# Prompt rows' down projection as seven half-size products, with differences of weight quarters prepared in the value and convolution stages

## What is computed

```
def ffn_sublayer(h, prev, g, w_gu, conv_w, conv_b, w_down):
    gate, up = jnp.split(rms_norm(h, g) @ w_gu, 2, axis=-1)
    gate_c, state = causal_dwconv3(gate, prev, conv_w)
    return h + (jax.nn.silu(gate_c + conv_b) * up) @ w_down, state
```

## Time and profile before

| | us |
| --- | --- |
| median of 3 runs | 1823.1 |
| lowest and highest run | 1813.66, 1824.73 |
| profiled execution | 1823.89 |
| its span, first to last instruction | 1822.1 |
| mean granted TensorE clock | 0.949 of full speed |

### The profile page before, as it was taken

How to read it: one execution, slowest core, us unless ns; L and a number is a source line. 1 busy time by engine, 2 the same in 40 slices (tenths; PEclk the granted TensorE clock), 3 DMA queues, 4 the chain that set the end, 5 groups by cost and what they waited for, 6 DMA issues and landing times.

```text
span 1822.1 us, 34225 instructions
## 1 busy us (share of the span) xinstructions
PE 1681.8 (92%) x13965; PEld 1179.9 (65%) x14043; DVE 1112.3 (61%) x1906; ACT 811.9 (45%) x1483; POOL 732.7 (40%) x704
## 2 busy tenths in 40 slices
PE   6999999997776889989979997999999999999998
PEld 3644444444444665445568654788888888898897
DVE  5856665788797875356745337888888878500000
ACT  5455478754533774342356325544444444301100
POOL 3232266888440110320033516666666666502200
PEclk9998899999787999989977999999999999999999
DMA  7031112122424110301253312112112112312311
GB/s 234 14 106 56 36 36 69 48 70 98 148 84 142 54 48 1 113 1 35 73 159 119 105 41 93 47 47 70 48 47 71 47 47 87 117 43 92 99 41 29
DMA packets 136550, 132.78 MB, mean 73 GB/s; under 512 B 15358, under 2 KB 109630, under 8 KB 136356
## 3 DMA queue, kind: packets, MB, share of 16 engines
q1 hardware_dynamic: 123850, 118.79, 21.1%
q10 hardware_dynamic: 12544, 11.80, 2.1%
HBM read 114.58 MB, written 15.98 MB: 72 GB/s over the span
## 4 chain that ended last, share of the span: by engine, by line
PE 70%; DVE 15%; ACT 7%; issue 4%; POOL 2%; DMA 2%; SPq 0%; ACTq 0%; DVEq 0%; POOLq 0%
PE PS L1611 23%; PE PS L1664 4%; PE PS L1665 4%; PE PS L1666 4%; PE PS L958 4%; PE PS L959 4%; PE PS L960 3%; ACT arena L1703 2%; PE PS L1155 2%; PE PS L1153 2%; ACT arena L1764 2%; PE PS L1154 2%; PE PS L1311 2%; PE PS L1323 1%; DVE arena L432 1%
## 5 line engine op out<-in xcount | busy, mean ns | idle before, releaser
L1611 PE MATMUL PS<-arena 128*128 128x272 f16 (+1 forms) x3696 | 429.9, 280 | 5.0 <-issue 5.0
L1611 PEld LDWEIGHTS PS<-arena 128*128 128x128 f16 (+1 forms) x3696 | 362.3, 98 | 72.8 <-issue 5.4
L1703 ACT ACTIVATE arena<-PS 128x512 f16<-128x512 f32 (+10 forms) x354 | 175.0, 523 | 176.6 <-PE PS L1323 41.4
L368 POOL TENSOR_TENSOR arena<-arena 128x512 bf16<-128x512 f32 (+2 forms) x144 | 161.3, 1154 | 189.8 <-ACT arena L359 189.5
L1703 ACT ACTIVATE arena<-arena 128x512 f16<-128x512 f32 (+5 forms) x214 | 136.0, 657 | 225.2 <-PE PS L1611 117.3
L958 PE MATMUL PS<-arena 128*128 128x512 f16 (+2 forms) x584 | 204.6, 361 | 8.1 <-POOL arena L368 3.5
L959 PE MATMUL PS<-arena 128*128 128x512 f16 (+2 forms) x584 | 204.3, 361 | 0.0
L1664 PE MATMUL PS<-arena 128*128 128x256 f16 x704 | 191.9, 273 | 1.4 <-POOL arena L936 1.0
L1665 PE MATMUL PS<-arena 128*128 128x256 f16 x704 | 191.9, 273 | 0.0
L1666 PE MATMUL PS<-arena 128*128 128x256 bf16 x704 | 191.9, 273 | 0.0
L960 PE MATMUL PS<-arena 128*128 128x512 bf16 (+2 forms) x544 | 188.0, 357 | 0.0
(11 more groups left out here) (363 smaller groups left out, 3777.8 us busy)
## 6 DMA issues: line engine op xcount, KB each, us to landing
arena<-w_gu SPq DMA_DIRECT2D x44, 512.0 KB, 5.0
arena<-w_down SPq DMA_DIRECT2D x8, 1408.0 KB, 7.2
arena<-w_in SPq DMA_DIRECT2D x8, 1024.0 KB, 6.2
arena<-w_kv_mem SPq DMA_DIRECT2D x8, 1024.0 KB, 7.0
arena<-cache_mem_k SPq DMA_DIRECT2D x32, 256.0 KB, 3.6
arena<-cache_mem_v ACTq DMA_DIRECT2D x28, 256.0 KB, 5.0
arena<-w_in SPq DMA_DIRECT2D x24, 256.0 KB, 3.7
arena<-x_prompt SPq DMA_DIRECT2D x9, 512.0 KB, 6.4
```

The source lines that it names most:

```text
L368: x = e.tensor_tensor(self.low(n)[:, 4 * half + k, :], wst[half][:, k, 0:width], self.high(n)[:, 4 * half + k, :], ALU.subtract)
L1611: mm = e.matmul(PS[:, product_bank(f, i) + c, 0:TC], w[:, i, k], s[i][:, q, c, :], start=first, stop=last)
L1703: e.activation(out, in_, ACT.Copy, **kw).then_inc(sem(name), 1)
```

## The change

The prompt part of the down projection, activations A (1024 x 2816) times w_down B (2816 x 1024), is cut into quarters: A by token half and by half of the 2816 (`KH` = 11 blocks of 128), B by the same half of the 2816 and by output column half. Seven products of quarter size (Winograd's form of Strassen's scheme) take the place of eight. The left factors are A11, A12, A22, and four sums made from the quarters; the right ones quarters B11, B21 and B22 and four differences of quarters.

- **Products.** `DOWN` lists seven products P1, P5, P2, P6, P4, P7, P3, each with four token tiles of 128 rows x 512 columns x 11 row blocks x three matmuls; P6 and P7 accumulate in PSUM on top of P1. Four of them carry a pass for the sample tokens (66 matmuls of 256 columns each).
- **Differences of weight quarters.** For each of eleven row blocks k, GpSimd makes four differences of 128 x 512 (`sums_of`), ScalarE rounds them (`sum_hi`), GpSimd makes the low halves (`lows_of`), and SP stores both to DRAM (`sum_store`); the weights come with `sum_load`, two row blocks ahead. There is one buffer for the rounded halves: `sum_hi(k)` waits for the stores of k - 1. Blocks 0 to 3 are rounded in the value stage, 4 to 6 between it and the convolution stage, 7 to 10 within that stage. The load of the memory tokens is moved behind the eleven stores.
- **Sums of activation quarters.** `left_sum` (VectorE), `left_hi` (ScalarE), `left_lo` (GpSimd) in 44 steps, spread over the first six products (`STEP_ENDS`). `ffn_high` writes the lower left quarter in float32 for it.
- **Right factors in the down stage.** Differences come back from DRAM (`sums_load`); quarters for P2 and P3 are loaded in pieces of 128 x 512, rounded by ScalarE (`right_hi`) and split by GpSimd (`right_lo`).
- **Output.** Residual quarters are loaded into `c_sum` (128 x 4 tiles x 512, four times), VectorE adds each PSUM tile to one or two of them (`down_sum`), and SP stores quarters of 1 MB, the last one tile by tile.
- The transposes of the states are cut into 16 and 6, within P1.

```diff
+            def sum_load(k):
+                if k >= 2:
+                    e.wait_ge(sem("tw_lo"), upto("tw_lo", 4 * (k - 1)))
+                for kh in range(2):
+                    e.dma_start(tw_in[k % 2][:, kh, :, :].rearrange("p a b -> p (a b)"),
+                                w_down[(kh * KH + k) * P:(kh * KH + k + 1) * P, :]).then_inc(sem(f"tw_ld{k % 2}"), 16)
+            def sum_store(k):
+                e.wait_ge(sem("tw_lo"), upto("tw_lo", 4 * (k + 1)))
+                for to, x in zip(tw_dram, (tw_hi, tw_lo)):
+                    e.dma_start(to[:, :, k, :].rearrange("i p n -> p i n"), x[:, :, :]).then_inc(sem("tw_st"), 16)
...
+            def sum_hi(k):
+                if k == 0:
+                    e.wait_ge(sem("s2_mm"), NI1)
+                else:
+                    e.wait_ge(sem("tw_st"), upto("tw_st", 32 * k))
+                for q in range(4):
+                    e.wait_ge(sem("tw_sum"), upto("tw_sum", 4 * k + q + 1))
+                    copy(tw_hi[:, q, :], tw_in[k % 2][:, T_AT[q] // 2, T_AT[q] % 2, :], "tw_hi")
+            SUM_HI_AT = {4: 7, 7: 8, 9 + 5: 9, 18 + 5: 10}
             for m in range(ND):
...
+                for j in range(value_done(m - 5), value_done(m - 4)):
+                    if j % 2:
+                        sum_hi(j // 2)
...
+            sum_hi(4)
             sign_step()
+            sum_hi(5)
             sign_step()
+            sum_hi(6)
             for x, item in enumerate(L4):
...
+                if x in SUM_HI_AT:
+                    sum_hi(SUM_HI_AT[x])
...
+            def sums_of(k):
+                v = tw_in[k % 2]
+                b11, b12, b21, b22 = v[:, 0, 0, :], v[:, 0, 1, :], v[:, 1, 0, :], v[:, 1, 1, :]
+                e.wait_ge(sem(f"tw_ld{k % 2}"), upto(f"tw_ld{k % 2}", 32 * (k // 2 + 1)))
+                for q, (out, a, b) in enumerate(((b11, b12, b11), (b12, b22, b12), (b22, b22, b11), (b21, b21, b22))):
+                    if q:
+                        e.wait_ge(sem("tw_sum"), upto("tw_sum", 4 * k + q))
+                    e.tensor_tensor(out, a, b, ALU.subtract).then_inc(sem("tw_sum"), 1)
+            def lows_of(k):
+                for q in range(4):
+                    e.wait_ge(sem("tw_hi"), upto("tw_hi", 4 * k + q + 1))
+                    e.tensor_tensor(tw_lo[:, q, :], tw_in[k % 2][:, T_AT[q] // 2, T_AT[q] % 2, :], tw_hi[:, q, :],
+                                    ALU.subtract).then_inc(sem("tw_lo"), 1)
             for j in range(NT):
...
+                if j % 2 == 0:
+                    sums_of(j // 2)
+                else:
+                    lows_of(j // 2)
+            lows_of(4)
+            for k in (5, 6):
+                sums_of(k)
+                if k < 6:
+                    lows_of(k)
             for f in range(NC_T):
                 A.split_lo(e, A_CONV + f + 1)
+                for k in ((6, 7), (8,), (9,), (10,))[f]:
+                    lows_of(k)
+                    if k + 1 < KH:
+                        sums_of(k + 1)
                 e.wait_ge(sem("s4_ev"), last_of[f] + 1)
```

The down stage, TensorE and VectorE (the old `down_tile`, `down_samples` and the loop at L2916 to L2923 go):

```diff
+        P1, P5, P2, P6, P4, P7, P3 = range(7)
+        LEFT = [(f11_hi, f11_lo), (x1_hi, x1_lo), (f12_hi, f12_lo), (f11_hi, f11_lo), (f22_hi, f22_lo), (x1_hi, x1_lo),
+                (f11_hi, f11_lo)]
+        CHAIN = (P1, P6, P7)
+        BANKS = [(6, 7, 2, 3) if i in CHAIN else (4, 5, 0, 1) for i in range(7)]
+        C11, C21, C12, C22 = range(4)
+        ADDED = [(C11,), (C12, C22), (C11,), (C12,), (C21,), (C21, C22), (C12,)]
+        STEP_ENDS = [0, 11, 17, 22, 28, 37, 44, 44]
...
+            def down_tile(i, t, first):
+                (xh, xl), wh, wl, cols = LEFT[i], z_hi[i % 2], z_lo[i % 2], slice(t * P, (t + 1) * P)
+                out = PS[:, down_bank(i, t), :]
+                for k in range(KH):
+                    if first:
+                        left_ready(i, k)
+                        right_ready(i, k)
+                    e.matmul(out, xh[:, k, cols], wh[:, k, :], start=(k == 0 and i not in (P6, P7)), stop=False,
+                             skip_group_check=i in CHAIN)
+                    e.matmul(out, xl[:, k, cols], wh[:, k, :], start=False, stop=False, skip_group_check=i in CHAIN)
+                    mm = e.matmul(out, xh[:, k, cols], wl[:, k, :], start=False, stop=(k == KH - 1),
+                                  skip_group_check=i in CHAIN)
+                mm.then_inc(sem("sw_mm"), 1)
...
+                if a == 0:
+                    link(e.tensor_tensor(s, s, f22_hi[:, k, :], ALU.add))
+                    e.tensor_tensor(s, s, f22_lo[:, k, :], ALU.add).then_inc(sem("as_sum"), 1)
...
+            for w in range(6):
+                first, steps = STEP_ENDS[w], STEP_ENDS[w + 1] - STEP_ENDS[w]
+                for k in range(KH):
+                    for n in range(first + steps * k // KH, first + steps * (k + 1) // KH):
+                        left_sum(n)
+                    if w > 0 and k in (4, 7, 9):
+                        down_sum(w, (4, 7, 9).index(k))
+                for t in range(0 if w == 0 else 3, 5 if w in SAMPLES else 4):
+                    down_sum(w, t)
+            for t in (4, 0, 1, 2, 3):
+                down_sum(P3, t)
```

More of the change, by code:

```diff
@@ new lines, in bank_used, with item_end, piece @@
+        def bank_used(n):
+            return max([m + 1 for m in range(n) if down_bank(*DOWN[m]) == down_bank(*DOWN[n])] or [0])
+        def item_end(i):
+            return max(n + 1 for n, it in enumerate(DOWN) if it[0] == i)
+        PIECES = [(i, k) for i in (P2, P3) for k in range(KH)]
+        W_BLOCK = {P2: (1, 0), P3: (1, 1)}
+        NPIECE = len(pieces)
+        T_AT = (0, 1, 3, 2)
+        TW = {P5: 0, P7: 1, P6: 2, P4: 3}
+        def piece(i, k):
+            return pieces[PIECES.index((i, k)) % NPIECE]
@@ L906, in _ @@
-            down_store(e, DOWN_ENDS[3], ND2)
-            e.wait_ge(sem("ffnst_ev"), upto("ffnst_ev", 1))
+            for half in range(2):
+                e.wait_ge(sem("fw_sum"), upto("fw_sum", 5 * FT))
+                e.wait_ge(sem("fw_lo"), 7 * (FT - 1) + ((M5 if half == 0 else M7) + 1))
+                ks = first_half(half)
+                e.dma_start(dst[:, ks.start:ks.stop, :],
+                            w_down[ks.start * P:ks.stop * P, 0:512].rearrange("(k p) n -> p k n", p=P)
+                            ).then_inc(sem(f"dw_ld{half}"), 16)
@@ L910, in _ @@
+            store_samples(e, 1)
+            for t in range(4):
+                e.wait_ge(sem("sw_ev"), item_end(P7) + 2 + t)
+                store_block(e, C12, t, t + 1)
             e.wait_ge(sem("st_out"), 64)
[L911 to L912 removed]
+            e.wait_ge(sem("y_st"), 16 * (3 + 4 + 4))
             for k in range(2):
@@ new lines, in down_samples @@
+            def down_samples(i, first):
+                k0, wh, wl = SAMPLES[i][0], z_hi[i % 2], z_lo[i % 2]
+                for k in range(KH):
+                    if first:
+                        right_ready(i, k)
+                    for x, w in ((fs_hi, wh), (fs_lo, wh), (fs_hi, wl)):
+                        for g in range(2):
+                            mm = e.matmul(PS[g * NS:(g + 1) * NS, down_bank(i, 4), 0:256], x[:, k0 + k, :],
+                                          w[:, k, g * 256:(g + 1) * 256], start=(k == 0 and x is fs_hi and w is wh),
+                                          stop=(k == KH - 1 and w is wl))
+                mm.then_inc(sem("sw_mm"), 1)
@@ L1685, in _, with turn_ffn_states @@
+            def turn_ffn_states(first, end):
+                for f in range(first, end):
+                    t = e.transpose(PS[0:18, BANKS[P5][(f - first) // 4], (f % 4) * P:(f % 4 + 1) * P], g_state[:, f, :],
+                                    ident[:, :])
+                t.then_inc(sem("ffnst_tp"), 1)
+            for n, (i, t) in enumerate(DOWN):
                 if n == 0:
                     e.wait_ge(sem("fw_sum"), upto("fw_sum", 5 * FT))
-                if j < NB:
-                    down_tile(n, c, j)
-                else:
-                    down_samples(n, c)
```

411 lines of the change are left out of this document (261 added, 150 removed).

## The result

| us | before | after |
| --- | --- | --- |
| median | 1823.9 (4 runs, 1813.7 to 1828.6) | 1842.4 (4 runs, 1840.7 to 1843.8) |
| ratio, 95% interval | | 1.0109 (1.0065 to 1.0153) |
| profiled execution, its span | 1823.9, 1822.1 | 1843.8, 1842.0 |

What follows compares the result with a forecast made beforehand. It took TensorE to bound the down stage and a ring through GpSimd and ScalarE the convolution stage. Profiled 1823.9 - 30.4 + 30.8 = 1824.3, median 0.8 lower, so 1823 us; range 1804 to 1843.

Steps and rivals of the forecast that it cites:

- Down stage: Down projection: fewer, 512-column matmuls, evictions 7.12 us apart, 224 us instead of 254; sum -30.4 us.
- no wait over 1 us: Down stage: a sign of the forecast, that TensorE would have no wait above 1 us there.
- What was costed at nothing: Down stage: VectorE, ScalarE and GpSimd work and loads hide below TensorE's 28.5 us a product; 0 us.
- the term of 8 us: Value stage: GpSimd's differences come late, so relu and TensorE stand still; +8 us, between bounds of 0 and 25.
- the joint rate of the two engines: Value stage: VectorE and GpSimd together move 1.25 times what one does, so 100 us of work takes 80.
- a walk in which only three sets come late: Value stage, contended subtractions at 1.75 us: second, third and fourth sets of differences late by 2, 4 and 2 us.
- the forecast's term: Before the first convolution block: seventh and eighth sets' roundings, low halves and stores delay the last copies; +8.1 us.
- Turns: Convolution stage: weights, low halves, stores, rounding and GpSimd's block in sequence lengthen turns two to four; +6.6, +6.6, +1.5 us.
- Small terms left at nothing: Start before the value stage, the fourth block itself, and all from there to the first down product: 0 us each.
- The high bound of 51: Value and convolution stages: most the added work could cost, with value stage 25 us and stores 5 us; 51 us.
- my own case: Whole kernel: additions of 19 to 45 us against 30.4 off 1823, giving 1812 to 1838; chance 0.70.
- Full exclusion: Value stage rival: VectorE and GpSimd work runs in series, stage +25 us instead of 8, 1840 us; chance 0.18.

Runs made afterwards that it cites:

- e5: Changed kernel with rectified scores left in PSUM, so VectorE's accumulation reads one SBUF operand; all 88 GpSimd subtractions kept: 1823.7 us.
- e3: Kernel before plus only 32 two-operand GpSimd subtractions on idle buffers in the value stage: 1841.3 us, ratio 1.0122.
- e2: Changed kernel with GpSimd's 32 value-stage subtractions (first four sets) replaced by one-column writes; roundings, loads and stores stay: 1825.8 us.
- e8: Kernel before with only the rectified scores left in PSUM, nothing of the change: 1820.1 us, ratio 0.9997.
- e10: Kernel before plus 64 GpSimd memsets in the value stage, which write SBUF but read none: 1821.7 us, ratio 1.0007.
- e6: Changed kernel with sets 6 to 10 of the differences (40 of 88 subtractions) made by VectorE instead of GpSimd: 1825.1 us.
- e4: Changed kernel with only the first four of eleven sets of differences made; sets 4 to 10 not loaded, subtracted or rounded: 1811.3 us.
- e9: Changed kernel with PSUM scores and sets 6 to 10 on VectorE, plus ScalarE's roundings and VectorE's low halves swapping places, some stores later: 1815.2 us.
- e1: Changed kernel without making the differences: no loads, subtractions or roundings for them, stores carry zeros: 1784.7 us, ratio 0.9824.

## Why the forecast was wrong

**Down stage: right.** Evictions stand 7.12 or 7.13 us apart, as worked out (VectorE's timeline):

```profile
1695.48 0.69 DVE L3129 TENSOR_TENSOR arena<-PS,arena 128x512 f32<-128x512 f32 x1 [4.15 <-PE PS L1779]
1702.61 0.69 DVE L3129 TENSOR_TENSOR arena<-PS,arena 128x512 f32<-128x512 f32 x1 [5.11 <-PE PS L1779]
```

TensorE's only waits are 1.84 and 0.89 us. I had left 0.5 standing of the first (low halves, L1038) and had 0.9 for the second, so the claim "no wait over 1 us" missed by one wait, without effect on the sum. What was costed at nothing (left sums, roundings, low halves, loads) was hidden.

**Value stage: the step that failed.** The mechanism was named, and the demand was nearly right (a difference takes GpSimd 1.27 us in e5, not 1.16, which makes 2 us for 20); what was mis-sized is the term of 8 us, which measured 16.4, and in it the joint rate of the two engines. I took 1.25 from one burst of four 384-wide subtractions. The changed kernel has a steady state. VectorE's timeline and GpSimd's at 160 us:

```profile
159.76 11.86 DVE L2587 SCALAR_TENSOR_TENSOR arena<-arena,iwt 128x896 f32<-128x896 f32 x6
```

```profile
158.75 7.89 POOL L3201 TENSOR_TENSOR arena<-arena 128x512 bf16<-128x512 f32 x4
```

Six in 11.86 and four in 7.89 us: one of each every 1.98 us, where alone they take 1.18 and 1.16. That is 2.34 us of work in 1.98, a rate of 1.18. e3 gives the same: 1.28 + 1.27 alone (the latter from e5), one of each in 10.88 / 5 = 2.18 us, 1.17. The forecast's own sum with it is 100 / 1.18 = 85 us against 70: +15, and measured are +16.4. So neither my rate nor work in series (2.34 us a pair, +25) is what happens; the rate lies between them, nearer to mine, and the small step from 1.25 to 1.18 is worth 5 us of the 8.4 missed. It was also wrong to lower +10 to +8 by a walk in which only three sets come late: once VectorE is the bound, each microsecond of it counts. The last 1.4 us are not divided further. e2, e3, e5 with e8, and e10 show the cause.

The Trainium skill, SBUF — State Buffer, "Who interferes with whom", says that a VectorE instruction with two SBUF inputs contends with a GpSimd instruction that reads SBUF, not with one that only writes, and that one with a single SBUF input, outside its two-port modes, doesn't contend. e3 and e10 agree on the first (20 us against nothing), e5 on the second (1.28 us beside 1.16). That the loser is blocked for a whole instruction is what the short instructions show (2.41 us instead of 0.17, below); the times of the long pairs still don't add up in full: 1.98 us, not 2.34.

**Between value stage and first block: the forecast's term right, a second one missing.** The first convolution product divides this stretch. TensorE's rows of the changed kernel and of the kernel before, the first product last:

```profile
192.68 1.14 PE L1237 MATMUL PS<-arena 64*64 64x264 f32 x2 [4.12 <-DVE arena L2600]
...
208.18 0.58 PE L1255 MATMUL PS<-arena 128*128 128x512 f16 x1 [0.64 <-issue]
```

```profile
170.84 0.83 PE L1135 MATMUL PS<-arena 64*64 64x264 f32 x2 [0.68 <-DVE arena L2421]
...
186.04 0.58 PE L1153 MATMUL PS<-arena 128*128 128x512 f16 x1 [0.64 <-issue]
```

From the first product to the first block it is 36.5 us before and 44.4 after: +8.0, where 8.1 was forecast. e6, with sets 6 and 7 on VectorE, has 36.1 there, and e4 35.8. That this is GpSimd's and ScalarE's work on two sets is so shown; one of its waits is for a store, longer than the 4 us that I had for a pair, but it holds GpSimd's low halves too (ScalarE's timeline):

```profile
250.23 2.19 ACT L1830 ACTIVATE arena<-arena 128x512 f16<-128x512 f32 x4 [7.54 <-DMA tw_lo_scratch<-arena]
```

The missing term is ahead of the first product: 21.8 us from the last relu's end instead of 18.1, +3.7. TensorE waits there for VectorE, 4.12 us instead of 0.68, because the last accumulations and the mask's addition behind them (1.23 us instead of 0.29) still run beside GpSimd's subtractions. In e3 and e4, where these end about 2 us after the last relu, the wait is 2.06 and 1.95 us. It is the exclusion of the value stage once more, and I had put it at nothing.

**Turns: right but for 1.2 us.** Forecast were 39.8, 39.8 and 34.7 us, measured are 39.7, 41.0 and 34.4. The cause is shown by e4 (33.2 without sets 7 to 10) and by e6 (33.9, 35.5, 36.8 with VectorE doing them).

**Small terms left at nothing.** The fourth block (+2.4) is the exclusion a third time. One of VectorE's search instructions, six columns wide, falls beside GpSimd's first product of the block (368.00, 2.34 us) and takes 2.41 us where it takes 0.17 when GpSimd is idle. ScalarE's search step waits for it, the scaled taps come behind that step, and GpSimd waits 5.99 us for them instead of 3.54. This is read from rows; in e4, without sets 7 to 10, the wait is 3.54 and the block 18.3 us:

```profile
367.95 2.41 DVE L2658 SCALAR_TENSOR_TENSOR arena<-arena 128x6 int32<-128x6 int32 x1
```

```profile
376.98 2.52 POOL L3236 TENSOR_TENSOR arena<-arena 128x1104 f32<-128x1104 f32 x1 [5.99 <-ACT arena L1830]
```

The two terms of +2.1, at the start and behind the fourth block, are not shown to be the change's. The first value copy starts at 98.78 in the changed kernel, where the granted clock from 90 to 100 us was 0.73, and at 95.73 and 95.75 in e3 and e4, where it was 0.93. From the rotary work to the first down product it is 1226.7 us in e10 and 1230.5 in e3, both with the kernel before's instructions there. So of the 19.6 us by which the shift exceeds the forecast's 30.8, the exclusion has 14.5 (8.4 in the value stage, 3.7 behind it, 2.4 in the fourth block) and differences between executions up to 4.2. The high bound of 51 for the added stages held 50.4, but my own case's range ended at 45; that the time still lies inside the range to 1843 is luck.

**The chances.** "Full exclusion" had 0.18 and ended at 1840; the time is 1842.4. It came near by another sum: the value stage grew by 16.4 us, not by 25, and terms that this rival left out made up the rest. It deserved more all the same: of a bound of 0 to 25 I took a third, on a rate read from a single burst of four instructions, and let it stand against a rule that named this very pairing.

## What to carry to other kernels

Before giving GpSimd two-operand work beside VectorE, add both engines' times and divide by 1.2, as measured here (1.17 and 1.18), not by 2: idle time of GpSimd is no room if VectorE reads two SBUF operands then. Short VectorE instructions count too: one of 0.17 us beside a GpSimd instruction cost 2.4 us here, because another engine waited for it. The cure is to take one operand from PSUM (e5), or to give the work to the faster engine where it idles (e6). And idle time inside a ring of engines is not room either: e9 filled it and lost 9 us.

## What the runs showed of the hardware that I had not expected

TensorE's granted clock can fall behind the value stage, for 16 to 20 us, in one run and not in another, with the same instructions on TensorE and the same busy share (9.3 of 10 us) in both (windows under e1). e10, whose TensorE list is that of the kernel before, kept the clock in its profiled run:

```profile
170.00:180.00 10.00, 9.23 (x32) 2.92 (x30) 4.74 (x13) 3.53 (x7) 0.00 (x0) 1.00 0.37 102
```

It is worth 8.9 us between the last relu and the first block (54.5 against 45.6). The times of the kernel before lie from 1813 to 1828 us, and this fall is large enough for most of that spread. Of its 27 executions beside e5 nine took 1813.5 to 1815.5 us at a mean granted clock of 0.954 to 0.959, and the other 18 took 1819.1 us or more, all but one at 0.953 or less. What triggers it stays open. Because of it a profile of one execution can be 9 us off in one stage; the table of parts holds only since both profiles had the fall.
